# Sums of weight blocks in another order, one copy moved, and a spatial gate in whole float32

## What is computed

```python
h = rms_norm(x, norm_mix_pre)
z = h @ w_in                                   # 1024 -> 10 x 1024
y_a = a_b * causal_dwconv(a_c * a_h, conv_a_w) # 3 taps
y_c = silu(layer_norm(causal_dwconv(c_a * sigmoid(c_g), conf_dw_w) + conf_dw_b))  # 31 taps
v = layer_norm(gelu(s_v)).reshape(b, s // 128, 128, 8, 128)
mixed = einsum("hts,bcshd->bcthd", tril(sgu_ws), v) + transpose(sgu_b)
y_s = gelu(s_u) * mixed                        # the spatial gate
m = (sigmoid(g_a) * (y_a @ w_branch[0]) + sigmoid(g_c) * (y_c @ w_branch[1])
     + sigmoid(g_s) * (y_s @ w_branch[2])) @ w_out
x = x + rms_norm(m, norm_mix_post)
h = rms_norm(x, norm_ffn_pre)
f = square(relu(h @ w_ff1)) @ w_ff2            # 1024 -> 4096 -> 1024, the MLP
x = x + rms_norm(f, norm_ffn_post)
```

## Time and profile before

| | |
|---|---|
| median of 3 runs | 974.44 us (973.62 to 975.53) |
| the profiled execution | 975.48 us, span 973.7 us |
| TensorE busy | 958.7 us (98%) |
| VectorE, ScalarE, GpSimd busy | 716.7 us, 422.6 us, 121.6 us |
| share of the chain that ended last | PE 93%, DMA 4%, DVE 1%, ACT 1% |
| moved by DMA | 140.23 MB |

### The profile page before, as it was taken

The page is one execution under the profiler, slowest core; times in us unless marked ns, Lnnn a source line. Parts: engine busy times, 40 slices in busy tenths (PEclk is TensorE's granted clock), DMA queues, the critical chain, the costliest instruction groups (busy, mean ns, idle before and its releaser), DMA issues.

```text
span 973.7 us, 13543 instructions
## 1 busy us (share of the span) xinstructions
PE 958.7 (98%) x4910; PEld 818.9 (84%) x4910; DVE 716.7 (74%) x839; ACT 422.6 (43%) x526; POOL 121.6 (12%) x146
## 2 busy tenths in 40 slices
PE   9999999999999999999999999999989999999997
PEld 7888888888888888888888888899779989989985
DVE  5458889889888898886585434598865785696698
ACT  5333332333333222223364323367735745754673
POOL 1100000001000001112200000132212112111112
PEclk9999999999999999999999999999999999999999
DMA  6323222232232222224325323469989979989765
GB/s 244 98 87 131 92 92 92 88 112 92 90 109 87 87 82 91 86 87 130 105 90 216 109 92 116 180 157 216 292 218 224 221 199 238 195 195 256 145 176 147
DMA packets 39196, 140.23 MB, mean 144 GB/s; under 512 B 4464, under 2 KB 4592, under 8 KB 39152
## 3 DMA queue, kind: packets, MB, share of 16 engines
q1 hardware_dynamic: 28608, 101.88, 30.3%
q0 software_dynamic: 9728, 34.61, 19.5%
q10 hardware_dynamic: 816, 3.15, 0.9%
HBM read 135.43 MB, written 4.19 MB: 143 GB/s over the span
## 4 chain that ended last, share of the span: by engine, by line
PE 93%; DMA 4%; DVE 1%; ACT 1%; issue 0%; POOL 0%; SPq 0%; DVEq 0%; ACTq 0%; POOLq 0%
PE ps L1449 25%; PE ps L1451 25%; PE ps L1453 25%; PE ps L1616 5%; PE ps L1620 5%; PE ps L1618 5%; DMA glu<-units_in 2%; DMA raw_d<-units_in 2%; PE ps L1523 1%; DVE w_lo L962 1%; PE ps L1492 1%; ACT w_hi L610 1%; PE ps L1557 0%; PE ps L1558 0%; PE ps L1556 0%
## 5 line engine op out<-in xcount | busy, mean ns | idle before, releaser
L1449 PE MATMUL ps<-a_hi,w_hi 128*128 128x512 f32 x576 | 225.4, 391 | 0.0
L1451 PE MATMUL ps<-a_lo,w_hi 128*128 128x512 f32 x576 | 224.2, 389 | 0.0
L1453 PE MATMUL ps<-a_hi,w_lo 128*128 128x512 f32 x576 | 224.1, 389 | 0.0
L962 DVE TENSOR_TENSOR w_lo<-raw,w_hi 128x1024 fp32r<-128x1024 f32 x124 | 153.1, 1238 | 89.2 <-ACT w_hi L610 89.0
L610 ACT ACTIVATE w_hi<-raw 128x1024 fp32r<-128x1024 f32 x124 | 130.2, 1056 | 189.8 <-PE ps L1453 119.1
L1038 DVE SCALAR_TENSOR_TENSOR conf<-glu,cols,conf (+1 forms) x240 | 187.0, 779 | 27.5 <-DVE conf L1038 26.4
L1451 PEld LDWEIGHTS ps<-a_lo,w_hi 128*128 128x128 f32 x576 | 108.2, 188 | 22.6 <-issue 0.5
L1449 PEld LDWEIGHTS ps<-a_hi,w_hi 128*128 128x128 f32 x576 | 108.1, 188 | 22.7 <-DVE w_lo L962 0.2
L1453 PEld LDWEIGHTS ps<-a_hi,w_lo 128*128 128x128 f32 x576 | 108.1, 188 | 22.5
L962 DVE TENSOR_TENSOR w_lo<-glu,w_hi 128x1024 fp32r<-128x1024 f32 x56 | 67.8, 1223 | 37.3 <-ACT w_hi L610 37.1
L1449 PE MATMUL ps<-w_hi,h_hi 128*128 128x512 f32 x224 | 88.5, 395 | 4.3 <-DVE w_lo L962 3.6
(11 more groups left out here) (175 smaller groups left out, 1663.4 us busy)
## 6 DMA issues: line engine op xcount, KB each, us to landing
raw<-units_in SPq DMA_DIRECT2D x128, 512.0 KB, 3.3
glu<-units_in POOLq DMA_DIRECT2D x40, 512.0 KB, 6.5
glu<-units_in SPq DMA_DIRECT2D x24, 512.0 KB, 5.1
raw_d<-units_in POOLq DMA_DIRECT2D x24, 512.0 KB, 7.9
raw_v<-units_in SPq DMA_DIRECT2D x16, 512.0 KB, 6.0
raw_d<-units_in SPq DMA_DIRECT2D x8, 512.0 KB, 4.0
conf<-x_in SPq DMA_DIRECT2D x4, 512.0 KB, 4.7
conf<-x_in ACTq DMA_DIRECT2D x1, 2048.0 KB, 7.8
```

The costliest lines, as they stand in the source:

```text
L962: return nc.vector.tensor_tensor(dst, src, hi, ALU.subtract)
L1449: nc.tensor.matmul(ps[:, bank, :], left_hi, right_hi, start=first, stop=False, skip_group_check=on_top)
L1451: nc.tensor.matmul(ps[:, bank, :], left_hi, right_lo, start=False, stop=False, skip_group_check=on_top)
L1453: return nc.tensor.matmul(ps[:, bank, :], left_lo, right_hi, start=False, stop=final, skip_group_check=on_top)
```

## The change

Three things are changed.

1. GpSimd's sums. The next quarter's UP 5 moves from ahead of DOWN 6 to between DOWN 7 and DOWN 4. In the first quarter DOWN 5 moves from behind UP 4 to ahead of it. SyncE's load of DOWN 5 in the first quarter waits for the sum of UP 6 instead of UP 7, and its load of UP 5 of the second quarter now waits for the sum of DOWN 6.
2. In the first quarter ScalarE copies the second half of UP 5's result, and splits the block behind it, before it rectifies h22.
3. The spatial gate's small products take whole float32 operands: one copy `v_tile` in place of `v_hi`, `v_lo`, and `ws_raw` in place of `ws_hi`, `ws_lo`. 5 matmul calls stand in place of 14.

```diff
-        v_hi = sb("v_hi", [P, CH, P], F32R)
-        v_lo = sb("v_lo", [P, CH, P], F32R)
+        v_tile = sb("v_tile", [P, CH, P])
+        room = sb("room", [P, 6 * P])
...
             for q in range(QUARTERS):
+                if q == 1:
+                    behind_sums(0, DOWN, 6)
                 if q:
                     for product in (5, 1, 2, 3):
                         ff_load(q, UP, product)
                 for product in (5, 1, 2, 3):
                     if q == 0 and product in (5, 1):
-                        behind_sums(0, UP, {5: 7, 1: 4}[product])
+                        behind_sums(0, UP, {5: 6, 1: 4}[product])
                     ff_load(q, DOWN, product)
...
             for q in range(QUARTERS):
                 add_block(q, UP, 6)
                 add_block(q, UP, 7)
-                add_block(q, UP, 4)
                 if q == 0:
                     add_block(0, DOWN, 5)
+                add_block(q, UP, 4)
+                add_block(q, DOWN, 6)
+                add_block(q, DOWN, 7)
                 if q < QUARTERS - 1:
                     add_block(q + 1, UP, 5)
-                for product in (6, 7, 4):
-                    add_block(q, DOWN, product)
+                add_block(q, DOWN, 4)
                 if q < QUARTERS - 1:
                     add_block(q + 1, DOWN, 5)
...
-                copy_hi(v_hi[:, :, :], by_token[:, :, bass.ds(j.times(P), P)]).then_inc(v_hi_ready, 1)
-                act.wait_ge(ws_masked, j.times(1, 1))
-                copy_hi(ws_hi[:, :], ws_raw[:, b, :]).then_inc(ws_hi_ready, 1)
+                nc.scalar.activation(v_tile[:, :, :], by_token[:, :, bass.ds(j.times(P), P)],
+                                     ACT.Copy).then_inc(v_tile_ready, 1)
...
                 done(q, UP, 5, 0)
                 keep(q, 5, "11", 0)
                 split_behind(q, UP, 5, 0)
-                act.wait_ge(joined, 5 * q + 1)
-                rectify(q, 1, "22", 1.0)
+                if q:
+                    act.wait_ge(joined, 5 * q + 1)
+                    rectify(q, 1, "22", 1.0)
                 done(q, UP, 5, 1)
                 keep(q, 5, "11", 1)
                 split_behind(q, UP, 5, 1)
+                if q == 0:
+                    act.wait_ge(joined, 1)
+                    rectify(q, 1, "22", 1.0)
...
-                dve.wait_ge(v_hi_ready, j.times(1, 1))
-                lo(v_lo[:, :, :], by_token[:, :, bass.ds(j.times(P), P)], v_hi[:, :, :]).then_inc(v_lo_ready, 1)
-                dve.wait_ge(ws_hi_ready, j.times(1, 1))
-                lo(ws_lo[:, :], ws_raw[:, b, :], ws_hi[:, :]).then_inc(ws_lo_ready, 1)
...
-                    pe.wait_ge(v_lo_ready, j.times(1, 1))
-                    pe.wait_ge(ws_lo_ready, j.times(1, 1))
-                    out = ps[:, 7, 0:P]
-                    nc.tensor.matmul(out, ones[:, :], ws_hi[:, :], start=True, stop=False)
-                    nc.tensor.matmul(out, ones[:, :], ws_lo[:, :], start=False, stop=True)
+                    pe.wait_ge(v_tile_ready, j.times(1, 1))
+                    pe.wait_ge(ws_masked, j.times(1, 1))
+                    nc.tensor.matmul(ps[:, 7, 0:P], ones[:, :].bitcast(F32), ws_raw[:, b, :], start=True, stop=True)
                     for c in range(CH):
-                        out = ps[:, 6, c * P:(c + 1) * P]
-                        nc.tensor.matmul(out, v_hi[:, c, :], ws_hi[:, :], start=True, stop=False)
-                        nc.tensor.matmul(out, v_hi[:, c, :], ws_lo[:, :], start=False, stop=False)
-                        mm = nc.tensor.matmul(out, v_lo[:, c, :], ws_hi[:, :], start=False, stop=True)
+                        mm = nc.tensor.matmul(ps[:, 6, c * P:(c + 1) * P], v_tile[:, c, :],
+                                              ws_raw[:, b, :], start=True, stop=True)
```

More of the change, by code:

```diff
@@ L258, in build @@
         resid = conf_flat[:, :].rearrange("p (c n) -> p c n", c=CH)
-        v_hi = sb("v_hi", [P, CH, P], F32R)
-        v_lo = sb("v_lo", [P, CH, P], F32R)
+        v_tile = sb("v_tile", [P, CH, P])
+        room = sb("room", [P, 6 * P])
         ws_raw = sb("ws_raw", [P, 2, P])
-        ws_hi = sb("ws_hi", [P, P], F32R)
-        ws_lo = sb("ws_lo", [P, P], F32R)
         bs_row = sb("bs_row", [P, 2, P])
@@ L284, in build @@
         ps = ctx.enter_context(nc.psum_tensor("ps", [P, 8, 512], F32))
-        raw_v = over("raw_v", [P, 2, D], "v_hi")
+        raw_v = over("raw_v", [P, 2, D], "v_tile")
         raw_d = over("raw_d", [P, 2, D], "conf", 2 * D)
@@ L358, in build @@
         y_a_lo = sem("y_a_lo")
-        v_hi_ready = sem("v_hi_ready")
-        v_lo_ready = sem("v_lo_ready")
+        v_tile_ready = sem("v_tile_ready")
         ws_masked = sem("ws_masked")
-        ws_hi_ready = sem("ws_hi_ready")
-        ws_lo_ready = sem("ws_lo_ready")
         spatial_done = sem("spatial_done")
```

## The result

The changed kernel takes 996.0 us (993.8 to 999.83, six runs) against 975.55 us (973.62 to 976.81, six runs) for the kernel before: a ratio of 1.0212 (95% interval 1.0196 to 1.0228), slower by some 20.5 us. The forecast was 990.8 us with 976 to 996: the sign and the mechanism that decides are right, one step is wrong, the size is 5 us too small, and the median stands at the very top of the range.

A forecast was written before the change was run, and what follows sets the result against it. TensorE was taken as the bound, almost never without work. Spatial gate -3.4, first quarter +3.8, second and third +16.0 made +16.4 us: 990.8 us on the median of 974.44, range 976 to 996 (8 in 10).

The forecast's parts named there:

- the mechanism that decides: All quarters but the last: UP 5's two sums between DOWN 7 and DOWN 4 make DOWN 4 land 5.3 us later.
- Spatial gate: Spatial gate's small products: 10 float32 instructions at 0.11 us, a gain of 0.42 us a tile, 3.4 us for 8 tiles.
- DOWN 6 in the first quarter: First quarter: DOWN 6's sums issued 6 us or more earlier, removing its 3.0 us wait and 1.6 us of slow clock.
- UP 7: First quarter: a new wait near 675 before UP 7's second unit, up to 5.3 us less some slack, counted as covered.
- the first quarter: DOWN 4 begins at 727.7 against 725.49, 2.2 us later, plus 1.6 us for the clock: 3.8 us lost.
- Second and third quarter: Before DOWN 4: a wait of 6.4 us plus 1.6 us of slow clock, 8.0 us a quarter, 16.0 us together.
- The fourth: Last quarter: no UP 5 behind it, so no change.
- (1): Rival: DOWN 4's slack of about 1 us absorbs the overlapping extra sums; -6.7 us, 967.7 us; chance 0.13.
- (2): Rival: the waits come but stay at 2 to 3 us and the clock does not fall; 974 to 977 us; chance 0.11.
- (3): Rival: spatial gate's float32 products do not overlap their loads; +11.5 us in place of -3.4, 1006 us; chance 0.05.
- (4): Rival: SyncE's loads slow DOWN 6's sums; its wait and slow clock, 4.6 us, stay; near 995 us; 0.05 with others.
- The rule of round-robin: UP 3's loads finish before the last of the four sums, so DOWN 4 lands at 807.8: 1 us more each quarter.

The follow-up runs named there:

- The run that took most of the wait in UP 7 away: Changed kernel with, in the first quarter, DOWN 5's sums behind UP 4's and loads of DOWN 1, 2, 3 behind DOWN 5's sum: 993.76 us, ratio 1.0197.

## Why the prediction was right and where it was wrong

**Spatial gate: right.** -3.4 forecast, -3.6 in the trace, -3.5 by itself. The price of 0.11 us an instruction, taken from the transposes, was right: 1.03 us for 10. The four passes of the Trainium skill ("FP8 and Floating Point Precision", section TensorE Precision Notes) had been turned into 2.16 us a tile, and the trace has 1.03. That doesn't speak against the passes but against their price of 0.11 us, which is the spacing of a whole small instruction. With 512 columns a float32 product takes 0.86 us where a float32r matmul takes 0.23, 3.7 times as long. A pass of 128 columns at that rate is some 0.06 us, and four passes for each of five products make 1.15 us, as an estimate; so the trace agrees with four passes. That the weight load sets the rhythm of small matmuls, as the forecast had it, no run tested.

**DOWN 6 in the first quarter: right.** Its sums are issued at 683.04 and 685.48 (forecast 684.9, or some 2 us later), and its wait and slow clock, 4.6 us, are gone.

**UP 7: the step that failed.** The forecast saw the wait ("up to those 5.3 us less some slack") and then struck it out: "It is covered by what follows: the end of the quarter is set elsewhere". The chain of after goes through it (start us, us):

```profile
664.48 9.84 DMA glu<-units_in
674.39 1.06 ACT w_hi L608
675.48 1.23 DVE w_lo L963
676.71 0.61 DVE h L1282
677.36 0.58 PE ps L1609
```

TensorE waits 5.2 us and then runs at the lower clock. Part of that is absorbed by small waits that the kernel before had there. But at DOWN 3 TensorE is 0.5 us later than before (704.67 against 704.19) instead of 3.6 us earlier, so 4.1 us of it are left. The split of DOWN 3 waits for TensorE to free a place in the ring, and DOWN 7's sums wait for that split. They are issued from 703.50. The forecast had said 703.25 "at about the same time", but in a count that had the 3.6 us of the spatial gate apart: on that count it was to be 699.9, and it came 3.6 us late. The whole crowd of six sums starts by that much later, and so does DOWN 4: at 727.38, which is 5.5 us late on the same count, against 2.2 forecast. With 1.5 us for the clock (forecast 1.6) the first quarter cost 7.0 us instead of 3.8. That the 727.7 us forecast for DOWN 4 and the 727.38 us of the trace look alike is luck: the forecast took off the 3.4 us of the spatial gate apart, so on its count the trace was to show 724.3. The run that took most of the wait in UP 7 away issued DOWN 7's sums from 699.36 and put DOWN 4 at 723.59, 1.7 us late on that count, where the forecast for the undisturbed queue was 2.2. The run with DOWN 5 behind UP 4 changed the order too but kept a wait of 5.7 us, and there DOWN 4 stayed late. So these 3.2 us are shown to come from the wait called covered. A wait ahead of the queue's crowd isn't hidden by the crowd; it moves the crowd.

**Second and third quarter: mechanism right, clock mis-sized.** In the second, DOWN 4's last block was to land at 806.8; it landed at 810.45, which is 807.1 after taking off the 3.4 us by which the quarter began later. The wait was to be 6.4 us and is 6.2. The clock was to cost 1.6 us and cost 2.5 to 2.7: behind the wait the slow stretch lasted 5.6 us where 3.6 had been read in the earlier trace rows. The three waits of like length show how: the lower level is as long in each, but in the second quarter only 1.4 us of it fell into the wait, in the others 3.6 to 3.9. That the third quarter's 1.6 us came out as forecast is luck in this sense, for its stretch was twice as long as that of the earlier trace rows and half of it was hidden. Together 9.0 instead of 8.0 us. In the third, 6.3 and 1.6 us make 7.9 against 8.0. The fourth changed nothing, as forecast.

The sum is -3.6 + 7.0 + 9.0 + 7.9 = 20.3 against 16.4; the spans differ by 20.2. The two errors of size, 3.2 and 1.0 us, make the difference. The median is 5.2 us above the forecast instead of 3.9 because the forecast was laid on 974.44 us, the median of three runs before, and the six runs before have 975.55.

**The rivals.** (1) fell: the queue doesn't overlap sums, it spaces them 2.5 us apart. (2) fell for the change, but is what half of it would have been (2.0 and 2.3 us), except that its point "the clock does not fall" failed there as well. (3) fell with 1.03 us a tile. (4) fell, no wait before DOWN 6. The rule of round-robin (the Trainium skill, "DMA: Bandwidth & Descriptors", section Queues, rings and completion order) was read as 807.8 with both loads of UP 3 done before the last sum. The row of after is 807.1 on the same count, and one load lands before the last sum (807.59), the other with it (810.61 against 810.45). Holding UP 3's loads took 2.6 to 2.8 us off a wait, near the whole of what these two loads were priced at (3 us). Both agree with sharing between the queues, though no run shows in which steps they share.

## What to carry to other kernels

On a queue that serves in order of issue, put a prefetch behind every transfer that is needed sooner, and price its place at the queue's own service time (here 2.5 us a sum alone, 3.8 us beside loads) for whatever stands behind it. This kernel's one line was worth some 24 us. When a stall is to be struck out as "covered by what follows", first ask whether the start of what follows hangs on the engine that stalls. And when a step is made to end sooner, look at which transfers it releases and whom they slow.

## What the runs showed of the hardware

- Sums onto SBUF, 0.5 MB each, land in the order of issue, 2.5 us apart alone and 3.8 us apart beside two loads. A single sum beside a dense row of loads took 12.0 to 12.2 us.
- How much the clock takes back doesn't follow the length of the wait. It fell just behind a wait of 2.0 us, and did not behind two of 3.4 us. Waits of 6.2 to 6.3 us cost 1.5, 2.5 and 1.6 us: the lower level lasted some 6.8 us in each, but began 3.9, 1.4 and 3.6 us before TensorE went on, and only what lay beyond the wait was paid for. It stayed up where the waits were filled with products that compute nothing. What sets the moment at which it falls was not found.
- True float32 products of 128x128 with 128 columns take 0.11 us an instruction, as the float32r ones do. So 5 calls, 10 instructions, do what 14 did in 1.51 us, in 1.03 us.
